# A four-layer hybrid trunk in split fp32: weight remainders and channel sums of the convolution moved to accumulating DMAs, its layer norm shifted by the mean of six blocks within the last block, and several splits reordered

## The chip, the cores and the metric

The kernel runs on one core of one Trainium2 chip. The metric is the device time of one execution in microseconds (us), median of several; less is better. The profile is one execution of its own.

## The reference, cut to what matters

Four layers over 528 tokens (16 meta tokens and 512 of the sequence) of 1024 channels. Each adds a mixer and a gated FFN to `h`; layers 0 and 3 mix by trailing means ("pool"), layer 1 by differential attention, layer 2 by a convolution with a layer norm, which most of the change is about:

```python
def conformer_conv(h, w_in, b_in, dw_w, dw_b, ln_g, ln_b, w_out, b_out):
    a, gate = jnp.split(h @ w_in + b_in, 2, axis=-1)
    u = a * jax.nn.sigmoid(gate)
    u = jnp.pad(u, ((0, 0), (CONV_WIDTH - 1, 0), (0, 0)))          # 31 taps, causal, per channel
    u = lax.conv_general_dilated(u, dw_w[:, None, :], window_strides=(1,), padding='VALID',
                                 dimension_numbers=('NWC', 'WIO', 'NWC'),
                                 feature_group_count=D_MODEL) + dw_b
    u = jax.nn.silu(layernorm(u, ln_g, ln_b))                     # mean and variance over 1024 channels
    return u @ w_out + b_out
...
for i in range(DEPTH):
    h = h + mixer(rmsnorm(h, norm_mix_g[i]))
    h = h + swiglu_ffn(rmsnorm(h, norm_ffn_g[i]), ffn_w_gate[i], ffn_w_up[i], ffn_w_down[i])
return rmsnorm(h[:, N_META:], final_norm_g)
```

## The kernel before

Activations lie transposed in SBUF: 8 blocks of 128 channels by 528 tokens (`h`, `y_hi`, `y_lo`, `cv`). Each fp32 product is made of three matmuls on rounded halves (hi x hi, hi x lo, lo x hi), so every weight tile (128 x 1024, in a ring of four slots) goes four steps: SyncE loads it into `w_raw` (L580), ScalarE rounds it into `w_hi` (`split_hi`, L1532), VectorE writes the remainder `w_raw - w_hi` into `w_lo` (`split_lo`, L1923, counted by `lo_ready`), and TensorE uses it (`chunk`, L834, counted by `tile_used`). SyncE reloads a slot once its `lo_ready` has come, ScalarE writes `w_hi` once TensorE has used the tile before.

The order of the work on each engine is written out by hand, and each engine runs its own program in order. For the convolution (`conv_in`, 8 channel blocks, 2 tiles each) the programs are, per block c:

- TensorE (`pair_layer`): two tiles of matmuls for block c+1, the second after `cv_ready` says that VectorE has read the banks of block c-1, then `convolve(c)` (L948): `TENSOR_TAPS` taps as banded matmuls, 6 per step, taps + 1 steps.
- VectorE (`conv_block`): the two `split_lo` for the next block; `cv_gate` and `cv_a` out of PSUM (L2521, L2523); `u` (L2526); the other 31 - 16 = 15 taps as one multiply-add each (L2534 to L2540, n = 0 to 14, even n into `cv`, odd n into `cv_odd`); `u_lo` behind n = 3 (L2544); behind n = 9 `add_products` of the block before (L2510, L2513), which counts `cv_ready`; at last cv + cv_odd (L2551). The last block has 20 taps on TensorE and 11 on VectorE.
- ScalarE (`conv_gate`): two `split_hi`, `swap_odd` of an earlier block (L1865), the diagonal tap matrices, two instructions of 64 columns per tap (L1852), the sigmoid (L1856), `u_hi` (L1859).
- GpSimd: adds each finished `cv` block into `cv_sum` (L811), seven times.

Layer norm: TensorE sums `cv_sum` and the eighth block over the channels (L1488, L1492), VectorE makes the mean and subtracts it from the eight blocks (L2565), ScalarE squares them (L1544), TensorE sums the squares per token by matmuls with one column (`sum_squares`, L861; two pairs of squares are added on VectorE first), VectorE makes the reciprocal root (L1968 to L1981), TensorE spreads it over the partitions (L868), VectorE copies it (`rstd`, L1986) and scales the blocks (L2577), ScalarE makes silu and `cv_hi`, VectorE `cv_lo` (L2573), and TensorE starts `conv_out`. `fill(n)` issues n matmuls whose result nobody reads, while TensorE would wait.

In the pool layers TensorE multiplies five tiles of rows with the weights (`rows_times_weights`, L892), ScalarE and VectorE split the results (`z_hi` L1591, `z_lo` L2050), and band matmuls (`windows`, L925 to L932) take the trailing means, which VectorE adds to `h` (L2024). In pool0 ScalarE adds a bias to the eight blocks of `h` (L1579), two behind each of the first four `z_hi`.

## Time and profile before

| | us |
|---|---|
| median of 3 runs | 2093.11 (2092.19 to 2095.8) |
| the profiled execution, its own time | 2090.65 |
| its span, first to last instruction | 2088.7 |

TensorE is busy in 97% of the span, VectorE in 76%, ScalarE in 41%, GpSimd in 11%. TensorE's clock is granted at full speed in most of the span and at half of it in some stretches; the mean is 0.983. The stages in order: pool0 until about 73, FFN 0 until 428, attention until 741, FFN 1 until 1094, the convolution until 1326, FFN 2 until 1689, pool3 until 1740, FFN 3 and the output until the end. A row of the timeline is one instruction, or several alike (x2), with start and duration; in brackets stands how long its engine had been idle before it and who ended that.

### The profile page before, as it was taken

To read this page: it belongs to the slowest core of one execution; us is meant where nothing else is said; L and a number is where in the kernel's file an instruction comes from. 1 tells how busy PE (TensorE), PEld (TensorE's weight loads), DVE (VectorE), ACT (ScalarE), POOL (GpSimd) and SP (SyncE) were. 2 spreads that over 40 slices of the span, in tenths; PEclk is the share of its full clock that TensorE was granted. 3 is DMA by queue.
4 is the path that set the end of the run, shared out by engine and by line. 5 is a ranking of instruction groups with operands and counts; after the bars stand their busy time and mean duration, and the time that the engine had idled before them with its cause. 6 is when DMAs were issued, how large, how long until landed. Compare 5 with 4: busy or idle time off the path is not lost.

```text
span 2088.7 us, 40727 instructions
## 1 busy us (share of the span) xinstructions
PE 2030.6 (97%) x16046; PEld 1957.5 (94%) x16046; DVE 1595.3 (76%) x2289; ACT 864.8 (41%) x1359; POOL 221.1 (11%) x309
## 2 busy tenths in 40 slices
PE   7999999999998999999999999999999999999998
PEld 6999999989886999999998999999999988999997
DVE  6797778767777579777978996587787867977794
ACT  6443334334444234333446554243443433433342
POOL 5100000412211400000050001100000061000000
PEclk8999999999998999999999999999999989999999
DMA  5333333331121132333332121223423422333332
GB/s 162 127 88 101 94 107 96 90 110 51 51 60 51 52 91 84 104 96 100 96 107 62 41 61 41 81 82 102 120 84 97 118 76 62 101 101 100 100 102 91
DMA packets 301914, 184.86 MB, mean 89 GB/s; under 512 B 6666, under 2 KB 297483, under 8 KB 301540
## 3 DMA queue, kind: packets, MB, share of 16 engines
q1 hardware_dynamic: 299932, 175.08, 29.2%
q10 hardware_dynamic: 1192, 4.34, 0.5%
q0 software_dynamic: 672, 3.80, 0.5%
q8 instruction: 82, 1.34, 0.3%
q14 instruction: 36, 0.29, 0.0%
HBM read 179.44 MB, written 6.44 MB: 89 GB/s over the span
## 4 chain that ended last, share of the span: by engine, by line
PE 85%; DVE 7%; DVEq 4%; ACT 2%; issue 2%; SPq 0%; DMA 0%; ACTq 0%
PE ps L834 42%; PE ps L1095 35%; DVEq L2539 3%; PE ps L1206 2%; DVE cv L2540 1%; PE ps L1297 1%; PE ps L1273 1%; DVE w_lo L1923 1%; PE ps L932 1%; PE ps L892 1%; DVE scores L2313 0%; PE ps L861 0%; PE ps L1284 0%; PE ps L1308 0%; DMA w_raw<-in_pool_w 0%
## 5 line engine op out<-in xcount | busy, mean ns | idle before, releaser
L1095 PE MATMUL ps<-t_lo,y_hi 128*128 128x264 f32 (+1 forms) x1008 | 285.7, 283 | 0.0
L1095 PE MATMUL ps<-t_lo,w_hi 128*128 128x264 f32 (+1 forms) x1008 | 285.7, 283 | 0.0
L1095 PE MATMUL ps<-t_hi,w_lo 128*128 128x264 f32 (+1 forms) x1008 | 285.4, 283 | 0.0
L1095 PE MATMUL ps<-t_hi,y_lo 128*128 128x264 f32 (+1 forms) x1008 | 285.3, 283 | 0.0
L1095 PE MATMUL ps<-t_hi,w_hi 128*128 128x264 f32 (+1 forms) x1008 | 285.1, 283 | 0.1
L1095 PE MATMUL ps<-t_hi,y_hi 128*128 128x264 f32 (+1 forms) x1008 | 284.8, 283 | 0.0
L834 PE MATMUL ps<-hid_hi,w_hi 128*128 128x264 f32 (+1 forms) x1184 | 265.2, 296 | 0.5 <-DVE hid_lo L2210 0.5
L834 PE MATMUL ps<-hid_lo,w_hi 128*128 128x264 f32 (+1 forms) x1184 | 264.7, 296 | 0.0
L1646 ACT ACTIVATE w_hi<-w_raw 128x1024 fp32r<-128x1024 f32 (+1 forms) x108 | 127.8, 1201 | 329.9 <-PE ps L834 193.6
L834 PE MATMUL ps<-hid_hi,w_lo 128*128 128x264 f32 (+1 forms) x1184 | 264.2, 296 | 0.0
L834 PE MATMUL ps<-y_hi,w_hi 128*128 128x264 f32 (+1 forms) x1088 | 246.3, 303 | 15.7 <-DVE cv L2513 9.2
L834 PE MATMUL ps<-y_lo,w_hi 128*128 128x264 f32 (+1 forms) x1088 | 236.6, 294 | 0.0
L834 PE MATMUL ps<-y_hi,w_lo 128*128 128x264 f32 (+1 forms) x1088 | 235.8, 294 | 0.0
L834 PEld LDWEIGHTS ps<-y_hi,w_hi 128*128 128x128 f32 x1088 | 172.7, 191 | 27.7 <-issue 14.8
L1646 ACT ACTIVATE y_hi<-w_raw 128x1024 fp32r<-128x1024 f32 (+1 forms) x108 | 125.8, 1196 | 166.6 <-DVE w_raw L2164 133.9
L834 PEld LDWEIGHTS ps<-hid_hi,w_hi 128*128 128x128 f32 x1184 | 187.2, 188 | 6.6 <-DVE hid_lo L2210 0.9
L834 PEld LDWEIGHTS ps<-hid_lo,w_hi 128*128 128x128 f32 x1184 | 187.6, 188 | 5.5
L834 PEld LDWEIGHTS ps<-hid_hi,w_lo 128*128 128x128 f32 x1184 | 187.4, 188 | 5.6
L1095 PEld LDWEIGHTS ps<-t_hi,w_hi 128*128 128x128 f32 x1008 | 189.8, 188 | 0.6 <-DVE h L2250 0.5
L1095 PEld LDWEIGHTS ps<-t_hi,y_hi 128*128 128x128 f32 x1008 | 189.8, 188 | 0.0
L1095 PEld LDWEIGHTS ps<-t_lo,w_hi 128*128 128x128 f32 x1008 | 189.5, 188 | 0.1
L1095 PEld LDWEIGHTS ps<-t_hi,w_lo 128*128 128x128 f32 x1008 | 189.5, 188 | 0.0
(315 smaller groups left out, 4435.0 us busy)
## 6 DMA issues: line engine op xcount, KB each, us to landing
w_raw<-in_ffn_w_gate SPq DMA_DIRECT2D x88, 512.0 KB, 5.1
w_raw<-in_ffn_w_up SPq DMA_DIRECT2D x88, 512.0 KB, 4.7
w_raw<-in_ffn_w_down SPq DMA_DIRECT2D x70, 512.0 KB, 4.3
w_raw<-in_ffn_w_down SPq DMA_DIRECT2D x24, 384.0 KB, 4.3
w_raw<-in_attn_w_qkv SPq DMA_DIRECT2D x16, 512.0 KB, 3.8
w_raw<-in_conv_w_in SPq DMA_DIRECT2D x16, 512.0 KB, 4.1
w_raw<-in_attn_w_qkv SPq DMA_DIRECT2D x16, 256.0 KB, 2.9
w_raw<-in_attn_w_o SPq DMA_DIRECT2D x8, 512.0 KB, 3.8
```

What stands on the lines that cost most here:

```text
L834: mm = pe.matmul(ps[:, bank + hf, 0:half], w[:, slot, col:col + P], x(hf), start=begin and w is m.w_hi and n == 0, stop=end and w is m.w_lo)
L892: mm = pe.matmul(out, y[:, at:at + rows], w[:, (t0 + g) % SLOTS, k * 256:(k + 1) * 256], start=k == 0 and n == 0, stop=k == 1 and n == 2)
L932: mm = pe.matmul(out[:, c0:c1], z, m.bands[0:TILE_ROWS[i], g, at:at + c1 - c0], start=i == 2 and n == 0, stop=i in (1, 4) and n == 1)
L1095: mm = pe.matmul(ps[:, bank, 0:hw], w[:, at:at + P], b[:, t, k, 0:hw], start=k == 0 and n == 0, stop=k == 3 and n == 2)
L1206: mm = pe.matmul(bank, x, w, start=False, stop=k == LAST_F - 1 and n == 2)
L1273: mm = pe.matmul(ps[:, (4, proj_banks(par, 1))[part] + c, col:col + k1 - k0], q[rows, q0:q0 + P], k[rows, k0:k1], start=n == 0, stop=n == 2)
L1297: pe.matmul(ps[:, 4, q0:QT * P], v[0:rows, vi, :], w, start=n == 0 and x == 0, stop=n == QT and x == 2)
L1646: act.activation(hi[:, sub * SUB:(sub + n_sub) * SUB], src, ACT.Copy).then_inc(s.op_hi, 1)
L1923: dve.tensor_tensor(m.w_lo[:, slot, 0:n], m.w_raw[:, slot, 0:n], m.w_hi[:, slot, 0:n].bitcast(F32), ALU.subtract).then_inc(s.lo_ready, 1)
L2539: dve.drain()
L2540: dve.scalar_tensor_tensor(out=sums[n % 2], in0=u, scalar=vec_col(ROW_DW + tap, c), in1=sums[n % 2], op0=ALU.mult, op1=ALU.add)
```

## The change

What it does, part by part:

1. **Remainders by DMA in `conv_in`** (16 tiles). ScalarE writes the negated rounded weights into `w_lo` (`negative_hi`), and GpSimd issues a DMA that adds `w_raw` to them (`add_raw`); it waits for both, and counts `lo_ready`. VectorE's `split_lo` is left out there (`split=False`).
2. **Channel sums by DMA.** GpSimd's adds into `cv_sum` become accumulating DMAs (`add_channels`), of six blocks; three pairs of squares are added likewise.
3. **Taps**: 15 on TensorE and 16 on VectorE in blocks 0 to 6 (16 and 15 before), 23 and 8 in the last (20 and 11 before). `add_products` stands behind n = 5.
4. **Layer norm**: the mean of blocks 0 to 5 is subtracted from blocks 0 to 6 within the last block (`centre_early`) and squared there by ScalarE; behind it block 7 is shifted, and an exact correction of variance and mean follows (`ln_factors`, `centre(c)` ahead of each scaling). TensorE's fills are 10 and 26.
5. **Around it**: in `conv_out` both first tiles of FFN 2 are split at block 6, one of them at block 7 before; in the last round of `down2` all four weight tiles of pool3 are split, two before.
6. **pool0**: TensorE takes the first three tiles of rows weight group by weight group; ScalarE has two of the eight biases between the `z_hi` and the rest behind them; some splits and the first `y_lo` stand elsewhere.

```diff
-TENSOR_TAPS = 16
-LAST_TAPS = 20
+TENSOR_TAPS = 15
+LAST_TAPS = 23
...
-LN_SINGLE = 4
-LN_SUMS = tuple(range(LN_SINGLE)) + tuple(range(LN_SINGLE, NB, 2))
+LN_EARLY = NB - 2
+LN_SUMS = tuple(range(0, LN_EARLY, 2)) + tuple(range(LN_EARLY, NB))
+SHIFTS0 = 32
...
@@ gpsimd @@
-            with pool.Fori(0, NB - 1) as d:
-                pool.wait_ge(s.cv_ready, d + 1)
-                pool.tensor_tensor(m.cv_sum[:, :], m.cv_sum[:, :], blk(m.cv, d), ALU.add).then_inc(s.cv_summed, 1)
-                pool.drain()
+
+            def add_channels(c):
+                pool.wait_ge(s.cv_ready, c + 1)
+                if c > 0:
+                    pool.wait_ge(s.cv_added, 16 * c)
+                pool.dma_start(m.cv_sum[:, :], blk(m.cv, c), accum_op=ALU.add).then_inc(s.cv_added, 16)
+            def add_raw(c):
+                for n in range(2):
+                    slot = (first["conv_in"] + 2 + n) % SLOTS if c % 2 == 0 else (first["conv_in"] + n) % SLOTS
+                    pool.wait_ge(s.negated, 2 * c + n + 1)
+                    pool.dma_start(m.w_lo[:, slot, :], m.w_raw[:, slot, :], accum_op=ALU.add).then_inc(s.lo_added[n], 16)
+                for n in range(2):
+                    pool.wait_ge(s.lo_added[n], 16 * (c + 1))
+                    pool.drain().then_inc(s.lo_ready, 1)
+            pool.wait_ge(s.lo_ready, first["conv_in"] + 2)
+            for c in range(NB):
+                add_raw(c)
+                if c > 1:
+                    add_channels(c - 2)
+            for d in range(0, LN_EARLY, 2):
+                pool.wait_ge(s.square_ready, squares_before(R_LN) + d + 2)
+                pool.dma_start(blk(m.cv_square, d), blk(m.cv_square, d + 1), accum_op=ALU.add)\
+                    .then_inc(s.square_pairs, 16)
...
@@ tensor: sum_squares @@
+                def columns_of(src, d, at, pitch):
+                    for n, t in enumerate((0, 128, 256, 384, TOK - P)):
+                        col = at + n * pitch
+                        mm = pe.matmul(ps[:, 5, col:col + 1], blk(src, d, t, P), m.ones[:, 0:1], start=True, stop=True)
+                    return mm
+                pe.wait_ge(s.square_pairs, 16 * (LN_EARLY // 2))
                 for j, d in enumerate(LN_SUMS):
-                    if d < LN_SINGLE:
+                    if d >= LN_EARLY:
+                        pe.wait_ge(s.cv_centred, d + 1)
+                        columns_of(m.cv, d, SHIFTS0 + d - LN_EARLY, 2)
                         pe.wait_ge(s.square_ready, squares_before(R_LN) + d + 1)
-                    else:
-                        pe.wait_ge(s.square_pairs, (d - LN_SINGLE) // 2 + 1)
-                    for n, t in enumerate((0, 128, 256, 384, TOK - P)):
-                        at = n * len(LN_SUMS) + j
-                        mm = pe.matmul(ps[:, 7, at:at + 1], blk(square, d, t, P), m.ones[:, 0:1], start=True, stop=True)
+                    mm = columns_of(square, d, j, len(LN_SUMS))
                 mm.then_inc(s.token_sums, 1)
+                for d in range(LN_EARLY, NB):
+                    for hf in range(2):
+                        mm = pe.matmul(ps[:, 2 + hf, 0:HALF], m.ones[:, :], blk(m.cv, d, hf * HALF, HALF),
+                                       start=d == LN_EARLY, stop=d == NB - 1)
+                mm.then_inc(s.cv_shifts, 1)
...
@@ tensor: pool_layer, rows of the first layer @@
-                    for i in range(TILES):
+                    for g in range(4):
+                        for i in range(3):
+                            rows_times_weights(i, (g,))
+                    for i in range(3, TILES):
...
@@ tensor: pair_layer, end of conv_in @@
+                    pe.wait_ge(s.cv_added, 16 * LN_EARLY)
+                    for hf in range(2):
+                        mm = pe.matmul(ps[:, hf, 0:HALF], m.ones[:, :], m.cv_sum[:, hf * HALF:(hf + 1) * HALF],
+                                       start=True, stop=True)
+                    mm.then_inc(s.cv_sums, 1)
...
@@ tensor: main @@
-            pe.wait_ge(s.cv_summed, NB - 1)
...
-            fill(22)
             sum_squares(m.cv_square)
-            fill(14)
+            fill(10)
...
@@ scalar @@
+            def negative_hi(t):
+                act.activation(m.w_lo[:, t % SLOTS, :], m.w_raw[:, t % SLOTS, :], ACT.Copy, scale=-1.0)\
+                   .then_inc(s.negated, 1)
...
-                for c in (2, 3):
-                    split_hi(tile0 + c, 0, 0, cols[tile0 + c])
                 if name == "pool0":
                     act.wait_ge(s.vec_ready, 1)
                     for d in range(NB):
                         y_hi(d, H_IN, Y_POOL0, ROW_MIX + 0, 0, TOK)
+                        if d in (1, 3):
+                            split_hi(tile0 + (3 + d) // 2, 0, 0, cols[tile0 + (3 + d) // 2])
...
-                    if i < TILES - 1 and name == "pool0":
-                        add_bias(2 * i)
-                        add_bias(2 * i + 1)
+                    if i in (1, 2) and name == "pool0":
+                        add_bias(i - 1)
                 for c in (4, 5):
                     split_hi(tile0 + c, 0, 0, cols[tile0 + c])
+                if name == "pool0":
+                    add_bias(2)
                 for d in range(NB):
                     y_hi(d, hn, yn, row, 0, TOK)
                     act.activation(blk(m.x_square, d), blk(m.h, d), ACT.Square).then_inc(s.square_ready, 1)
+                    if name == "pool0" and d + 3 < NB:
+                        add_bias(d + 3)
...
+                rounds(f"down{layer}", NB, 1, 2, lambda d: y_hi(d, hn, yn, row, 0, TOK),
+                       given={2: [(pool3 - 4, 512), (pool3 - 3, 512)], 3: [(pool3 - 2, 512), (pool3 - 1, 512)]}
+                       if layer == 2 else None)
...
-            rounds("conv_in", NB, 2, NB // 2, conv_gate, True)
+            rounds("conv_in", NB, 2, NB // 2, conv_gate, True, negate=True)
             act.wait_ge(s.conv_done, NB - 1)
             swap_odd(NB - 2, 0)
             for g in (2, 3):
                 split_hi(first["conv_out"] + g, 0, 0, SLOT)
+            squares(s.cv_centred, 0, m.cv, m.cv_square, 0, NB - 1)
             act.wait_ge(s.conv_done, NB)
             swap_odd(NB - 1, 1)
-            squares(s.cv_centred, 0, m.cv, m.cv_square)
+            squares(s.cv_centred, 0, m.cv, m.cv_square, NB - 1, NB)
...
-            rounds("conv_out", NB, 1, 2, conv_out, True, 2)
+            rounds("conv_out", NB, 1, 2, conv_out, True, 2, {2: [(first["up2"] - 4 + c, SLOT) for c in range(2)], 3: []})
...
@@ vector @@
-                for d in range(NB):
-                    if d < 2:
-                        split_lo(tile0 + 4 + d, 0, 0, cols[tile0 + 4 + d])
+                split_lo(tile0 + 4, 0, 0, cols[tile0 + 4])
+                add_windows(0)
+                split_lo(tile0 + 5, 0, 0, cols[tile0 + 5])
+                y_lo(0, yn, row, 0, TOK)
+                for d in range(1, NB):
                     add_windows(d)
-                    if d > 0:
+                    if d > 1:
                         y_lo(d - 1, yn, row, 0, TOK)
...
+                    return
+                pool3 = first["pool3"]
+                out_rounds(f"down{layer}", 1, 2, half, t0, None, yn, row, (0, 2, 4, 6),
+                           given={2: [(pool3 - 4, 512), (pool3 - 3, 512)], 3: [(pool3 - 2, 512)]},
+                           before_low=lambda: split_lo(pool3 + 3, 0, 0, 512))
...
+            def centre(c):
+                return dve.tensor_tensor(blk(m.cv, c), blk(m.cv, c), m.cv_mean[:, :], ALU.subtract)
+            def centre_early():
+                dve.wait_ge(s.cv_sums, 1)
+                dve.tensor_scalar(halves(m.cv_mean[:, :]), banks(0, HALF), 1.0 / (LN_EARLY * P), None, ALU.mult)
+                dve.drain()
+                for c in range(LN_EARLY + 1):
+                    centre(c).then_inc(s.cv_centred, 1)
+            def ln_factors():
+                n = 5
+                x, t = m.tok_x[:, 0:n], m.tok_t[:, 0:n]
+                dve.wait_ge(s.token_sums, R_LN + 1)
+                for sums, at, k in ((x, 0, len(LN_SUMS)), (t, SHIFTS0, NB - LN_EARLY)):
+                    dve.tensor_reduce(out=sums, in_=ps[:, 5, at:at + n * k].rearrange("p (n j) -> p n j", j=k),
+                                      axis=mybir.AxisListType.X, op=ALU.add)
+                dve.drain()
+                dve.tensor_scalar(x, x, 1.0 / D, LN_EPS, ALU.mult, ALU.add)
+                dve.scalar_tensor_tensor(out=t, in0=t, scalar=-1.0 / (D * D), in1=t, op0=ALU.mult, op1=ALU.mult)
+                dve.drain()
+                dve.tensor_tensor(x, x, t, ALU.add)
+                rsqrt(x, m.tok_r[:, 0:n], n)
...
+                dve.wait_ge(s.cv_shifts, 1)
+                dve.tensor_scalar(halves(m.cv_mean[:, :]), banks(2, HALF), 1.0 / D, None, ALU.mult)
+                dve.drain()
+                centre(0)
+                dve.wait_ge(s.rstd_sums, spreads(R_LN) + 1)
+                dve.tensor_copy(halves(m.rstd[:, :]), banks(6, HALF)).then_inc(s.rstd_ready, 1)
+                dve.drain()
...
-                    if n == 9 and not (isinstance(c, int) and c == 0):
+                    if n == 5 and not (isinstance(c, int) and c == 0):
                         add_products(c - 1, 1 - par)
+                        if isinstance(c, int) and c == NB - 1:
+                            dve.drain()
+                            centre_early()
...
-            rounds("conv_in", NB, 2, NB // 2, conv_block, conv_start)
+            rounds("conv_in", NB, 2, NB // 2, conv_block, conv_start, split=False)
             dve.drain()
             add_products(NB - 1, 1)
+            dve.drain()
+            centre(NB - 1).then_inc(s.cv_centred, 1)
+            dve.wait_ge(s.lo_ready, first["conv_out"] + 2)
             split_lo(first["conv_out"] + 2, 0, 0, SLOT)
-            dve.wait_ge(s.cv_sums, 1)
-            dve.tensor_scalar(halves(m.cv_mean[:, :]), banks(4, HALF), 1.0 / D, None, ALU.mult)
-            dve.drain()
-            for c in range(NB):
-                dve.tensor_tensor(blk(m.cv, c), blk(m.cv, c), m.cv_mean[:, :], ALU.subtract)\
-                   .then_inc(s.cv_centred, 1)
-            for d in range(LN_SINGLE, NB, 2):
-                add_squares(R_LN, d // 2, m.cv_square)
-            rstd_of(R_LN, LN_EPS, before_copy=lambda: split_lo(first["conv_out"] + 3, 0, 0, SLOT))
+            split_lo(first["conv_out"] + 3, 0, 0, SLOT)
+            ln_factors()
...
+                if c + 1 < NB:
+                    centre(c + 1)
+                    dve.drain()
...
-            out_rounds("conv_out", 1, 2, HALF, 0, ROW_CONV_OUT, Y_FFN2, ROW_FFN + 2, (0, 2, 4, 6), 2)
+            out_rounds("conv_out", 1, 2, HALF, 0, ROW_CONV_OUT, Y_FFN2, ROW_FFN + 2, (0, 2, 4, 6), 2,
+                       {2: [(first["up2"] - 4 + c, SLOT) for c in range(2)], 3: []})
```

## Rows read from the trace of the kernel before

**Rows 1.** The page, busy time of each engine.
```profile
PE 2030.6 (97%) x16046; PEld 1957.5 (94%) x16046; DVE 1595.3 (76%) x2289; ACT 864.8 (41%) x1359; POOL 221.1 (11%) x309
```

**Rows 2.** Busy by stretch (PE, PEld, DVE, ACT, POOL), then clock, DMA share, GB/s.
```profile
1103.40:1241.50 138.10, 128.78 (x1304) 125.89 (x1304) 126.70 (x173) 84.92 (x273) 9.00 (x6) 0.96 0.16 46
...
1173.00:1174.00 1.00, 1.00 (x6) 1.00 (x6) 1.00 (x1) 1.00 (x5) 1.00 (x1) 0.50 0.00 0
...
1241.50:1277.80 36.30, 33.68 (x340) 32.21 (x337) 29.57 (x56) 13.59 (x21) 2.41 (x2) 0.91 0.21 59
```

**Rows 3.** Timeline of VectorE, one block in the loop.
```profile
1180.95 0.71 DVE L2521 TENSOR_TENSOR cv_gate<-ps,rstd 128x528 f32<-128x528 f32 x1
...
1187.90 0.76 DVE L2540 SCALAR_TENSOR_TENSOR cv_odd<-cv_u,vec,cv_odd 128x528 f32<-128x528 f32 x1
...
1193.31 1.88 DVE L2540 SCALAR_TENSOR_TENSOR cv<-cv_u,vec,cv 128x528 f32 x1 [0.19 <-issue]
...
1199.12 2.35 DVE L1923 TENSOR_TENSOR w_lo<-w_raw,w_hi 128x1024 fp32r<-128x1024 f32 x2
1201.51 0.71 DVE L2521 TENSOR_TENSOR cv_gate<-ps,rstd 128x528 f32<-128x528 f32 x1
```

**Rows 4.** Timeline of GpSimd: the same block, and the issue of a DMA.
```profile
1193.30 1.32 POOL L811 TENSOR_TENSOR cv_sum<-cv_sum,cv 128x528 f32<-128x528 f32 x1 [19.23 <-DVE cv L2513]
...
1661.84 0.62 POOL L816 DMA_DIRECT2D bands<-bands_scratch  x1 [333.20 <-PE ps L834]
```

**Rows 5.** Timeline of TensorE, from about the same block.
```profile
1172.70 0.62 PE L834 MATMUL ps<-y_hi,w_hi 128*128 128x264 f32 x2 [1.93 <-DVE cv L2513]
...
1180.26 0.39 PE L948 MATMUL ps<-u_hi,tap_hi 64*128 64x264 f32 x2
...
1186.74 0.51 PE L834 MATMUL ps<-y_hi,w_hi 128*128 128x264 f32 x2
...
1193.26 0.51 PE L834 MATMUL ps<-y_hi,w_hi 128*128 128x264 f32 x2 [0.40 <-DVE cv L2513]
```

**Rows 6.** Timeline of ScalarE, the same block, and the last block's sigmoid.
```profile
1184.10 2.02 ACT L1532 ACTIVATE w_hi<-w_raw 128x1024 fp32r<-128x1024 f32 x2
...
1187.65 0.35 ACT L1852 ACTIVATE tap_hi<-diag,vec_hi 128x64 fp32r<-128x64 f32 x1
...
1195.09 0.34 ACT L1852 ACTIVATE tap_lo<-diag,vec_lo 128x64 fp32r<-128x64 f32 x1
...
1242.21 0.74 ACT L1856 ACTIVATE cv_sig<-cv_gate,vec 128x528 f32<-128x528 f32 x1 [3.73 <-DVE cv_gate L2521]
```

**Rows 7.** The view of DMA issues: KB each, us from issue to landing.
```profile
w_raw<-in_conv_w_in SPq DMA_DIRECT2D x16, 512.0 KB, 4.1
...
bands<-bands_scratch POOLq DMA_DIRECT2D x1, 1598.0 KB, 7.5
```

**Rows 8.** Timeline of TensorE and VectorE in the layer norm.
```profile
1260.51 8.60 PE L861 MATMUL ps<-ones,cv_square 128*128 128x1 f32 x60
...
1269.14 0.19 DVE L1968 TENSOR_REDUCE tok_x<-ps 128x5 f32<-128x30 f32 x1 [3.83 <-PE ps L861]
...
1273.87 0.71 DVE L1986 COPY rstd<-ps 128x528 f32<-128x528 f32 x1
...
1277.81 0.48 PE L834 MATMUL ps<-cv_hi,w_hi 128*128 128x264 f32 x2 [0.83 <-DVE cv_lo L2573]
```

**Rows 9.** TensorE at the start of FFN 2 (timeline).
```profile
1326.88 0.48 PE L834 MATMUL ps<-y_hi,w_hi 128*128 128x264 f32 x2 [2.04 <-issue]
```

**Rows 10.** TensorE's waits over the span: us in total, times, longest; here pool3.
```profile
PE ps L892 <- DVE w_lo L1923: 2.1, 2, 1.4
```

**Rows 11.** Timeline of pool0: TensorE, ScalarE, TensorE.
```profile
19.67 0.55 PE L892 MATMUL ps<-w_hi,y_hi 128*128 128x256 f32 x1 [5.36 <-DVE y_lo L1929]
...
27.90 1.35 ACT L1579 ACTIVATE h<-h,pool_bs 128x528 f32<-128x528 f32 x2
...
43.71 0.78 PE L834 MATMUL ps<-y_hi,w_hi 128*128 128x264 f32 x2 [0.31 <-DVE y_lo L1929]
```

78 lines of the change are left out of this document (36 added, 42 removed).

## The prediction

> **What bounds the kernel now.** I read the page first: TensorE is busy in 97% of the span [rows 1], so time can only come from stretches in which it waits, works at the lower clock, or does work that this change takes away. The busy time by stretch, read next, shows where the change works: the seven intervals between the gates of the eight convolution blocks take 138.1 us, or 19.7 each, and in them VectorE is busy 126.7 us, nearly as long as TensorE; the layer norm behind them takes 36.3 us until `conv_out` starts [rows 2].
>
> The timelines of one block say who leads. VectorE takes 20.56 us from gate to gate, with no wait but short drains [rows 3]. TensorE waits for VectorE's `add_products` in every block, 1.93 us in one and 0.40 in the next, and after the long wait its granted clock is 0.50, the 1.2 GHz level [rows 2, 5]. Its own work in a block is two tiles of 6.1 us each (6.52 less the wait of 0.40) and a convolution of 6.48 us, together 18.7 [rows 5]. So VectorE sets the pace, and its slack to TensorE is about 1.9 us a block.
>
> **The convolution blocks.** VectorE loses the two remainders, 2.39 us with their overhead (1199.12 to 1201.51) [rows 3]. It loses a stall too: the multiply-add behind `add_products` takes 1.88 instead of 0.76 us, and starts with GpSimd's add (1193.31, 1193.30; the add takes 1.32), so the add costs VectorE 1.12 us a block [rows 3, 4]. It gains one tap, 0.76. That gives 20.56 - 2.39 - 1.12 + 0.76 = 17.8 us. TensorE loses one step of 17 in the convolution, 0.38 us: 18.7 - 0.4 = 18.3. `add_products` moves from behind n = 9 to behind n = 5: at 7.7 us into the block (1188.66, the end of the row at 1187.90) and 1.3 us long it is over at 9.0, and TensorE asks for it 12.2 us in (6.1 of convolution, 6.1 of a tile). That wait goes, and the slow clock with it. What is late next is TensorE itself. From the first gate, two tiles (12.2) and six blocks of 18.3 make 122; VectorE's own, 138.1 - 7 x 2.39 - 6 x 1.12 + 7 x 0.76, would make 120 [rows 2, 3]. 122 against 138.1 is **-16 us**.
>
> What takes over the removed work: ScalarE gets two negations of about 1 us each (as the two roundings, 2.02) and gives back two tap instructions, 0.48. It has some 7 us of idle time ahead of a sigmoid in these blocks and 3.7 in the last one [rows 6], so seven blocks hide it. Its order costs little: `swap_odd` comes at about 7.9 us, ahead of the 8.6 at which the last third of `add_products` wants it. GpSimd's DMAs: nothing in this trace shows an accumulating one. From below they cost nothing, for they have from 7 us (both negated) until TensorE wants the tile in the next block at 18.3 + 6.1 = 24.4, that is 17 us, and nobody but SyncE's reload (4.1 us of slack use) is queued behind `lo_ready`. The nearest rows are a plain load of 512 KB, 4.1 us, and GpSimd's own of 1598 KB, 7.5 [rows 7]. If an accumulation moves twice the bytes, a pair takes 6 to 9 us: hidden. I take nothing. The wait that `add_raw` adds holds back only `add_channels` of two blocks before, which is wanted in the last block.
>
> The Trainium skill ("DMA: Bandwidth & Descriptors", Anatomy of one DMA) prices a DMA from GpSimd at 2.0 us and its bytes at 436 GB/s, an estimate of 3.2 us for 512 KB; it gives no price for adding. By it the sum stays as it is.
>
> **The last block and the layer norm**, counted from the gate of block 7; before: 36.3 us to the first matmul of `conv_out`. ScalarE is 3.4 us later with its taps (negations 2.0, six instructions more at 0.24, 1.4), and the interval is about 1.1 us shorter, against a slack of 3.73 [rows 6]: the sigmoid is about 0.8 late. n = 5 and `add_products` end at 9.0, mean and seven subtractions at 0.63 take 5.1 to 14.1, the last square but one is there at about 15, and the pair sums by DMA at 18 (3 us each, overlapping; between 2 and 7). TensorE, with 24 steps at 0.38 behind 6.9, is free at 16 and waits. It then has 35 column sums where it had 30; those took 8.6 us, 0.29 each, the early ones faster and the last at the lower clock [rows 8]. Block 7's square is there by 19, so TensorE bounds this too: 18 + 9 = 27, and before it was 27.6 (1269.14 less 1241.5). VectorE's two `split_lo` lie under it. From there to the copy of `rstd` it was 4.7 us; now a second reduction and the correction add 0.6, mean and subtraction of block 0 ahead of the copy add 1.4, and a `split_lo` that stood there leaves, its 1.2 having been partly hidden: 5.5. From copy to first matmul it was 3.9 [rows 8]; three more subtractions with drains on VectorE ahead of the first `cv_lo` add 2.1, less 0.35 of waiting: 5.6. 27 + 5.5 + 5.6 = 38.1, or **+2 us** with nothing for a lower clock at the start of `conv_out`. The same gap of 1 to 3 us on TensorE can cost that too: after 1.93 us of waiting the clock was at 1.2 GHz and the tile took 7.56 us (1172.70 to 1180.26) instead of 6.1, a loss of 1.4 [rows 2, 5]. Bounds: -3 (pair sums early, column sums at full clock) and +6.
>
> **FFN 2's start.** TensorE stood 2.04 us for the second tile, split after block 7's add [rows 9]. Split at block 6 it is there a whole block earlier, and TensorE has all else, so this goes whole: **-2 us** (0 if VectorE, which only adds and splits there, were late with it).
>
> **pool3.** Two waits for remainders, 2.1 us together [rows 10], go, and with them a slow clock behind them (up to 1.4 more). But next late is GpSimd's sum of squares, which starts late there, behind the landing of its own DMA. **-2 us**, between 0 and -4.
>
> **pool0.** Six of the eight biases, 1.25 us per two with the overlap taken off [rows 11], leave the chain of `z_hi`: 3.8 us. But the fifth `z_hi` needs TensorE's last row tile, and that comes earlier only by TensorE's earlier start: it stood until 19.67 for `y_lo` [rows 11], and VectorE comes to it about 1.8 us sooner. So the chain gives about 2; `y_lo` of block 0, ahead of the second window add and not behind it, gives about 1.5 more at 43.71, where TensorE waits for it [rows 11]. **-3.5 us**, between -1.5 and -5.5.
>
> **The sum**: -16 + 2 - 2 - 2 - 3.5 = -21.5. The profiled execution took 2090.65, so it would be 2069.2; the median of the runs lies 2.46 above it, which gives 2071.6.
>
> **The rivals.** (1) *The issues take VectorE's port as the add did.* GpSimd issues three DMAs a block, 0.62 us each by the one issue in the trace [rows 4]. If VectorE stands still for them as it did for the add [rows 3], its block is 17.8 + 1.9 = 19.7, 1.4 over TensorE's, seven times: +10, 2081. For it: the stall of 1.12 beside the add. Against it: the issue reads no tensor. The Trainium skill ("SBUF — State Buffer", Who interferes with whom) has VectorE's instructions with two SBUF inputs contend only with a GpSimd instruction that reads SBUF. By that rule this rival costs nothing, and the stall beside the add, which reads, agrees.
>
> (2) *Slower: the accumulating DMAs set the pace.* GpSimd runs them in one queue: a pair, its waits, then the channel sum, about a quarter of a pair's bytes. With 2 us for issues and drains a block takes 2 + 1.25 D, D being the pair. Hidden while D is under 13 us. The other parts save 5.5, so the kernel is slower than before once a block takes over 19.7 + 0.8 = 20.5, D = 15 us or 7.4 us a tile. At D = 20 a block takes 27, and the kernel is (27 - 19.7) x 7 - 5.5 = 45 us slower: 2139. For it: no accumulating DMA is in the trace, and none of 512 KB from SBUF to SBUF. Against it: 1598 KB in 7.5 us, and only 16% of the DMA engines used in the stretch [rows 2, 7].
>
> (3) *The convolution gives more*: if the 6.1 of a tile holds some slack and VectorE leads, the blocks give -19, and the layer norm nothing back: 2066.
>
> (4) *The early shift brings nothing or less*: pair sums late (each at 7 us) and a slow clock at `conv_out`, +6 instead of +2, and pool0 and pool3 give half: 2079.
>
> **How the numbers follow.** Forecast (2066 to 2077) 0.55; (1) 0.12; (3) 0.10; (4) 0.14; (2) 0.09, of which 0.03 is a D just about 14 us that ends within 0.2% of before. 0.2% is about what a measurement of this kernel can tell from no change. Faster 0.91, same 0.03, slower 0.06. The range goes from 2063 (rival 3 with pool0 at its best) to 2084 (rival 1 with half of the small gains).
>
> **What would show it.** Gate to gate at 18.0 to 18.6 us, TensorE without waits for `cv` in the blocks and its clock at 1.0; multiply-adds of VectorE all at 0.77 (1.2 or more beside an issue: rival 1); accumulations of 512 KB landing in 3 to 6 us, and no wait of TensorE for `w_lo` (over 7 us: rival 2); gate of block 7 to `conv_out` at 36 to 40 us, column sums ending at about 27. The prediction fails if an accumulating DMA is much slower than a plain one, or if TensorE in the shorter blocks meets a wait that is hidden now.

## The result, and the profile after

The changed kernel takes 2074.24 us (median of 4 runs, 2073.35 to 2076.54) against 2092.65 of the kernel before: a ratio of 0.9913, 95% interval 0.9896 to 0.993. The forecast was 2071.6, the range 2063 to 2084. Its profiled execution took 2073.5, span 2071.6 (before 2090.65 and 2088.7). In the profile the change is worth 17.1 us where 21.5 were forecast. The median hides 1.7 of that gap by luck: it lies 0.7 us above the profiled execution, where the forecast had added the 2.46 of the kernel before.

The total also hides errors that partly cancel: 8.5 us too little in one row, 4.1 more than forecast over the others. By the same instruction in both traces, in us ("products" are the matmuls of L1095 before and L1141 after, TensorE's longest runs in each FFN):

| stretch | before | after | difference | predicted |
|---|---|---|---|---|
| start to the first product of FFN 0 | 126.36 | 120.70 | -5.7 | -3.5 |
| FFN 0, attention, FFN 1, start of conv_in | 977.03 | 976.55 | -0.5 | 0 |
| gate of block 0 to gate of block 7 | 138.08 | 122.12 | -16.0 | -16 |
| gate of block 7 to conv_out's first matmul | 36.34 | 46.81 | +10.5 | +2 |
| conv_out, head of FFN 2, to its second products | 186.53 | 184.06 | -2.5 | -2 |
| rest of FFN 2, pool3, head of FFN 3, to its second products | 396.72 | 393.70 | -3.0 | -2 |
| sum | | | -17.1 | -21.5 |

The page, then busy time by stretch (columns as in [rows 2]): the blocks, the last block up to the end of its convolution, the column sums, and from there to `conv_out`.

```profile
PE 2022.0 (98%) x16010; PEld 1951.4 (94%) x16010; DVE 1578.2 (76%) x2287; ACT 878.4 (42%) x1367; POOL 233.4 (11%) x327
```

```profile
1097.25:1219.37 122.12, 120.62 (x1254) 118.79 (x1256) 108.97 (x165) 96.15 (x277) 17.10 (x20) 1.00 0.62 138
1219.37:1235.40 16.03, 16.00 (x242) 15.20 (x238) 14.08 (x23) 10.55 (x22) 2.57 (x3) 1.00 0.31 62
1239.05:1254.18 15.13, 15.13 (x71) 15.13 (x72) 1.90 (x3) 1.59 (x2) 0.00 (x0) 0.50 0.25 70
1254.18:1266.18 12.00, 9.26 (x48) 8.12 (x49) 9.88 (x29) 4.21 (x6) 0.54 (x1) 0.82 0.00 0
```

In the blocks TensorE is busy 120.6 of 122.1 us at clock 1.00, where it was busy 128.8 of 138.1 at 0.96 [rows 2]. Behind them, 15.1 us pass with TensorE at the 1.2 GHz level and VectorE all but idle (busy 1.9): there most of the loss against the forecast lies.

VectorE's wait in the first block, then one block of the loop (timeline; answers [rows 3]), and GpSimd's part in one; then the view of DMA issues.

```profile
1100.14 0.77 DVE L2611 SCALAR_TENSOR_TENSOR cv_u<-cv_a,vec,cv_sig 128x528 f32<-128x528 f32 x1 [1.56 <-ACT cv_sig L1904]
...
1166.83 0.71 DVE L2606 TENSOR_TENSOR cv_gate<-ps,rstd 128x528 f32<-128x528 f32 x1
1168.58 0.77 DVE L2611 SCALAR_TENSOR_TENSOR cv_u<-cv_a,vec,cv_sig 128x528 f32<-128x528 f32 x1 [0.42 <-ACT cv_sig L1904]
...
1174.47 0.87 DVE L2595 TENSOR_TENSOR cv<-ps,cv 64x264 f32 x2
...
1175.97 0.77 DVE L2625 SCALAR_TENSOR_TENSOR cv<-cv_u,vec,cv 128x528 f32 x1 [0.19 <-issue]
...
1184.80 0.71 DVE L2606 TENSOR_TENSOR cv_gate<-ps,rstd 128x528 f32<-128x528 f32 x1
```

```profile
1154.43 0.86 POOL L827 DMA_DIRECT2D w_lo<-w_raw  x1 [9.21 <-ACT w_lo L1584]
1156.32 0.86 POOL L827 DMA_DIRECT2D w_lo<-w_raw  x1 [1.03 <-ACT w_lo L1584]
1162.58 0.86 POOL L820 DMA_DIRECT2D cv_sum<-cv  x1 [5.40 <-DMA w_lo<-w_raw]
```

```profile
w_raw<-in_conv_w_in SPq DMA_DIRECT2D x16, 512.0 KB, 4.3
w_lo<-w_raw POOLq DMA_DIRECT2D x16, 512.0 KB, 5.4
...
cv_sum<-cv POOLq DMA_DIRECT2D x6, 264.0 KB, 6.6
cv_square<-cv_square POOLq DMA_DIRECT2D x3, 264.0 KB, 4.3
```

Gate to gate is 17.97 us where it was 20.56. Every multiply-add takes 0.77, the first one behind `add_products` too (1.88 before [rows 3]). An adding DMA of 512 KB lands in 5.4 us, and a pair is there 8.2 us after its first issue (1154.43 to 1162.58). The Trainium skill ("DMA: Bandwidth & Descriptors", Anatomy of one DMA), from which the prediction took an estimate of 3.2 us, falls short of it for an adding DMA; here the measurement decides, and the difference is hidden either way.

The layer norm, TensorE and VectorE (timeline; answers [rows 8]):

```profile
1239.05 6.56 PE L885 MATMUL ps<-ones,cv_square 128*128 128x1 f32 x30 [3.68 <-DMA cv_square<-cv_square]
1245.47 2.27 PE L885 MATMUL ps<-ones,cv 128*128 128x1 f32 x10
1247.60 2.27 PE L885 MATMUL ps<-ones,cv_square 128*128 128x1 f32 x10
1249.73 2.27 PE L885 MATMUL ps<-ones,cv 128*128 128x1 f32 x10
1251.87 2.27 PE L885 MATMUL ps<-ones,cv_square 128*128 128x1 f32 x10
1254.00 3.87 PE L898 MATMUL ps<-cv,ones 128*128 128x264 f32 x8
1254.18 0.18 DVE L2563 TENSOR_REDUCE tok_x<-ps 128x5 f32<-128x25 f32 x1 [13.23 <-PE ps L885]
1260.32 0.71 DVE L2580 COPY rstd<-ps 128x528 f32<-128x528 f32 x1 [0.90 <-PE ps L906]
1266.18 0.48 PE L862 MATMUL ps<-cv_hi,w_hi 128*128 128x264 f32 x2 [2.74 <-DVE cv_lo L2657]
```

The 35 column sums stand in 70 rows (two each), ten of which take 2.13 us from start to start: 0.43 us a sum. They start 19.7 us behind the gate of block 7 (1239.05 less 1219.37) and end at 34.6; the prediction had 18 and 27.

### The profile page after: what moved, and what is told of

The parts are those of the page before. It is cut to its first block, busy times and chain, and to the rows that moved or that the text cites. A ratio compares the mean times of both kernels' runs of the same rounds, so it can differ in the third digit from the quotient of the medians.

```text
span 2071.6 us, 40663 instructions
## 1 busy us (share of the span) xinstructions
PE 2022.0 (98%) x16010; PEld 1951.4 (94%) x16010; DVE 1578.2 (76%) x2287; ACT 878.4 (42%) x1367; POOL 233.4 (11%) x327
## 4 chain that ended last, share of the span: by engine, by line
PE 78%; DVE 8%; DVEq 4%; ACT 3%; issue 3%; POOLq 1%; DMA 1%; SPq 0%; ACTq 0%; POOL 0%
PE ps L862 38%; PE ps L1141 31%; DVEq L2624 2%; PE ps L1252 2%; PE ps L930 1%; PE ps L1343 1%; PE ps L1319 1%; DVE w_lo L1972 1%; PE ps L885 1%; PE ps L973 1%; DVE cv L2625 1%; DVE w_lo L2198 1%; DVEq L2234 1%; POOLq L750 1%; DVEq L2203 1%
## 5 line engine op out<-in xcount | busy, mean ns | idle before, releaser
L1141 PE MATMUL ps<-t_lo,y_hi 128*128 128x264 f32 (+1 forms) x1008 | 285.8, 284 | 0.0
L1141 PE MATMUL ps<-t_lo,w_hi 128*128 128x264 f32 (+1 forms) x1008 | 285.8, 284 | 0.0
L1141 PE MATMUL ps<-t_hi,w_lo 128*128 128x264 f32 (+1 forms) x1008 | 285.5, 283 | 0.0
L1141 PE MATMUL ps<-t_hi,y_lo 128*128 128x264 f32 (+1 forms) x1008 | 285.4, 283 | 0.0
L1141 PE MATMUL ps<-t_hi,w_hi 128*128 128x264 f32 (+1 forms) x1008 | 285.2, 283 | 0.0
L1141 PE MATMUL ps<-t_hi,y_hi 128*128 128x264 f32 (+1 forms) x1008 | 284.9, 283 | 0.0
L1141 PEld LDWEIGHTS ps<-t_hi,w_hi 128*128 128x128 f32 x1008 | 189.9, 188 | 0.6 <-DVE h L2294 0.5
L1141 PEld LDWEIGHTS ps<-t_hi,y_hi 128*128 128x128 f32 x1008 | 189.9, 188 | 0.0
L1141 PEld LDWEIGHTS ps<-t_lo,w_hi 128*128 128x128 f32 x1008 | 189.6, 188 | 0.1
L1141 PEld LDWEIGHTS ps<-t_hi,y_lo 128*128 128x128 f32 x1008 | 189.5, 188 | 0.0
L1141 PEld LDWEIGHTS ps<-t_hi,w_lo 128*128 128x128 f32 x1008 | 189.5, 188 | 0.0
```

The costliest lines, as they stand in the source:

```text
L1141: mm = pe.matmul(ps[:, bank, 0:hw], w[:, at:at + P], b[:, t, k, 0:hw], start=k == 0 and n == 0, stop=k == 3 and n == 2)
```

## The experiments

The distance that most runs turn on, from the gate of block 7 to the first matmul of `conv_out`, was read from each run's timeline:

| run | median, us | ratio to before, 95% | gate 7 to conv_out |
|---|---|---|---|
| before | 2092.65 | | 36.34 |
| changed | 2074.24 | 0.9913 (0.9896 to 0.993) | 46.81 |
| e1_fill_ahead | 2076.3 | 0.9925 (0.9909 to 0.9942) | 45.28 |
| e2_unpaired | 2074.63 | 0.9918 (0.9901 to 0.9934) | 46.95 |
| e3_chain | 2070.44 | 0.9901 (0.9885 to 0.9918) | 40.37 |
| e4_old_ln | 2065.44 | 0.9878 (0.9861 to 0.9894) | 37.80 |
| e5_split_vector | 2090.8 | 0.9992 (0.9983 to 1.0002) | 42.84 |
| e6_add_gpsimd | 2080.54 | 0.9943 (0.9927 to 0.996) | 44.60 |
| e7_taps14 | 2079.78 | 0.9945 (0.9927 to 0.9963) | 44.54 |
| e8_spread_old | 2080.73 | 0.9951 (0.9935 to 0.9968) | 45.72 |
| e9_dma_twice | 2083.27 | 0.9955 (0.9938 to 0.9971) | 43.45 |
| e10_keep_pool3 | 2062.81 | 0.9852 (0.9836 to 0.9869) | 39.26 |
| e11_keep_ln | 2062.06 | 0.9859 (0.9843 to 0.9876) | 37.65 |
| e12_early_few | 2067.84 | 0.9887 (0.9871 to 0.9904) | 43.09 |

The runs e5 to e9 have the changed kernel's layer norm as it is, and the distance still runs from 42.84 to 46.81 with it. Their column sums start 18.4 to 20.7 us behind the gate and take 11.3 to 15.0, by the instant at which the clock falls: e8, which starts them behind the same wait as the changed kernel (3.69 us), takes 13.6. Differences under 4 us there are not to be read as effects. Each group of runs was measured beside the kernel before, whose median moved between 2091.2 and 2092.7, so medians of different rows compare to some 1.5 us.

### The layer norm: where do the 10.5 us come from?

**e4_old_ln**: the changed kernel with the layer norm of before.

```diff
-LAST_TAPS = 23
+LAST_TAPS = 20
-LN_SUMS = tuple(range(0, LN_EARLY, 2)) + tuple(range(LN_EARLY, NB))
+LN_SUMS = tuple(range(LN_SINGLE)) + tuple(range(LN_SINGLE, NB, 2))
-                            centre_early()
+            add_channels(NB - 2)
...
```

> The changed kernel with the layer norm of the kernel before: mean of all eight blocks, 20 taps in the last block, six column sums a group, the channel sum still by DMAs. What the early shift costs or gives by itself. My prediction put it at +2 us of 38.3; the trace of the changed kernel has 46.8 from gate 7 to conv_out. If the early shift itself is the loss (theory A), this kernel takes 35.5 to 37.5 us there (36.3 in the kernel before, TensorE with one step less in block 6, ScalarE later with the taps) and the whole kernel is 9 to 11 us faster than the changed one: 2064. Rival E, the loss comes from what the other edits brought into that stretch (DMAs of GpSimd, the late sigmoid, the shorter block ahead of it): 42 us or more here too, and the kernel is no more than 5 us faster.

37.80 us, just over theory A's 37.5, and 8.8 us faster in the median. The early shift itself is the loss, and not what the other edits brought into the stretch (rival E wanted 42 or more).

```profile
1238.11 10.16 PE L887 MATMUL ps<-ones,cv_square 128*128 128x1 f32 x60
...
1256.98 0.48 PE L860 MATMUL ps<-cv_hi,w_hi 128*128 128x264 f32 x2 [0.83 <-DVE cv_lo L2663]
```

With the gate at 1219.18 its column sums end at 28.95 us (34.63 in the changed kernel, 5.7 later), and from there to `conv_out` it takes 8.85 (12.2, 3.3 more). So two thirds of the loss lies ahead of the last column sum and one third behind it.

**e1_fill_ahead**: matmuls that nobody reads fill the wait for the pair sums; 1.04 us of it are left behind them.

```diff
+            pe.wait_ge(s.cv_centred, 1)
+            fill(30)
             sum_squares(m.cv_square)
```

> The changed kernel, with 30 matmuls that nobody reads between the last convolution and the column sums, where TensorE stands 3.68 us for the pair sums. Counted from the gate of block 7 to the first matmul of conv_out (46.8 us in the changed kernel). Theory A, the lower clock after that wait is what costs: the clock stays at 1.0 into the column sums, they take 7 to 9 us where they took 15.1, and the interval is 39 to 41, the kernel 6 us faster. Rival B, column sums of one column let the clock fall whatever ran ahead of them: they take 14 us or more and the interval stays at 46 to 47.5. Rival C, they are slow for another reason than the clock (their own weight loads, the DMA beside them): the clock shows 1.0 and they still take 0.43 us each.

45.28. TensorE's clock, by slices (TensorE busy, clock, DMA share, GB/s):

```profile
1239.00:1242.00 3.00, 3.00 (x26) 1.00 1.02 172
1242.00:1246.00 4.00, 2.96 (x27) 1.00 0.28 73
1246.00:1250.00 4.00, 4.00 (x30) 0.75 0.66 198
1250.00:1254.00 4.00, 4.00 (x21) 0.50 0.00 0
```

The sums began at 1244.07 (20.9 us behind the gate, 1.2 later than in the changed kernel), at full clock, and lost it within 4 us although nothing interrupted them (TensorE is busy 4.00 of 4.00 us in both of the last slices); all 35 took 11.4 us instead of 15.0. At full clock a sum takes 0.22 us (the first 15 in 3.37). Neither theory A's 39 to 41 nor rival B's "14 us or more" came out, and rival C is excluded, for the duration follows the clock. A full clock ahead of the sums is kept for their first part only.

**e2_unpaired**: no pair sums by DMA, 50 column sums.

```diff
-            for d in range(0, LN_EARLY, 2):
-                pool.wait_ge(s.square_ready, squares_before(R_LN) + d + 2)
-                pool.dma_start(blk(m.cv_square, d), blk(m.cv_square, d + 1), accum_op=ALU.add)\
-                    .then_inc(s.square_pairs, 16)
-LN_SUMS = tuple(range(0, LN_EARLY, 2)) + tuple(range(LN_EARLY, NB))
+LN_SUMS = tuple(range(NB))
```

> The changed kernel without the three adding DMAs for the pairs of squares: TensorE sums the columns of all eight squares one by one, 50 column sums where it had 35, and has no DMA to wait for, so that it starts behind the last convolution, some 4 us earlier. Theory A (clock): from a start without a wait the sums run the first part at full clock, 0.21 us each, and then drop to 0.43; 50 of them at a mean of 0.3 are 15, and the interval from the gate of block 7 to conv_out is 43 (-4 us). Rival B (clock always low in these sums): 50 x 0.43 = 21.5 us from 16.5, the interval is 49.5 (+2.7). Rival D, the landing of the DMA is the whole loss: -3.7 us and more.

46.95, between theory A's 43 and rival B's 49.5. The sums began at 15.9 us, 3.75 earlier, and ended at 35.2: 19.2 us for 50, the clock at 0.50 from 1242 on. The DMA's landing is not the loss (rival D falls); what it bought, fifteen sums less, was worth just what its wait cost.

**e3_chain**: VectorE adds the squares of blocks 3 to 6 while it is idle.

```diff
+            for a, b in ((3, 4), (5, 6), (3, 5)):
+                e = dve.tensor_tensor(blk(m.cv_square, a), blk(m.cv_square, a), blk(m.cv_square, b), ALU.add)
-LN_SUMS = tuple(range(0, LN_EARLY, 2)) + tuple(range(LN_EARLY, NB))
+LN_SUMS = (0, 1, 2, 3, NB - 1)
```

> The changed kernel without the adding DMAs of squares; VectorE, which stands 13.2 us there, adds the squares of blocks 3 to 6 in three additions (2.1 us), and TensorE has 35 column sums as in the changed kernel, the first 25 without a wait right behind the convolution. Theory A (clock kept by an early start): sums from 16.5 us behind the gate, 35 x 0.25 to 0.3 = 9 to 10.5, done at 26 to 27 where the changed kernel is done at 34.6: the interval is 38 to 40 and the kernel 7 us faster. Rival B (clock low whatever comes ahead): 35 x 0.43 = 15 us from 16.5, done at 31.5, the interval 43.7, 3 us faster.

```profile
1235.29 4.02 PE L881 MATMUL ps<-ones,cv_square 128*128 128x1 f32 x30
1239.17 4.41 PE L881 MATMUL ps<-ones,cv 128*128 128x1 f32 x20
1243.43 4.41 PE L881 MATMUL ps<-ones,cv_square 128*128 128x1 f32 x20
```

40.37, just over theory A's 40. But the sums took 12.4 us, between its 9 to 10.5 and rival B's 15: the first 15 ran mostly at full clock, 3.9 us; the other 20 took 8.5, 0.43 each. 6.4 us came back, 3.7 of them from the earlier start and 2.5 from the clock. In the profile 3.0 us of that are lost again in pool3 (42.6 us there where the changed kernel has 39.6); e10 says why.

**e12_early_few**: the early shift with fewer sums, an early start, and the fills of pool3 (e10 below).

```diff
-LN_SUMS = tuple(range(0, LN_EARLY, 2)) + tuple(range(LN_EARLY, NB))
+LN_SUMS = (0, 1, 2, NB - 1)
...
+                        for _ in range(14):
+                            pe.matmul(ps[:, 0, 0:HALF], m.y_hi[:, 0:P], m.y_hi[:, 0:HALF], start=True, stop=True)
...
+            for a, b in ((2, 3), (4, 5), (2, 6), (2, 4)):
```

> The early shift of the changed kernel, with its column sums arranged as the runs so far suggest: VectorE adds the squares of blocks 2 to 6 (four additions, 2.9 us), TensorE has 30 column sums where the changed kernel has 35, starts them behind the last convolution, runs 14 matmuls that nobody reads ahead of the last ten; pool3 with the added matmuls as in the last two runs. Is the idea at fault or the way its sums are made? Theory (only the sums): they end 25 us behind the gate of block 7 (34.6 in the changed kernel, 28 in the run before), and with the 12.2 us that the changed kernel takes from there conv_out starts at 36 to 37, as early as with the old layer norm or earlier (37.65): about 2061 for the kernel. Rival (the early shift costs by its longer tail and by TensorE's own shift sums, whatever the squares do): 38.5 us or more, the kernel 1 us or more slower than the run before.

43.09, and 2067.84 against the 2062.06 of e11_keep_ln, which differs from it in the layer norm. The sums were done at 30.1 us, not at 25: this time the clock fell 2 us after they began (they start at 1237.88, and its mean from 1239 to 1242 is 0.64), and the 14 added matmuls took 3.2 us at the low clock. From the last sum to `conv_out` it took 13.0. The rival's number holds: even with 30 sums the early shift is behind the old form, which had 20 in e11 and 9.8 us from its last sum to `conv_out`. By these figures 3.2 us of the 5.4 between the two lie in the tail and 2.3 ahead of it.

### The blocks: who leads, and does the DMA hold?

**e5_split_vector**: the remainders back on VectorE, nothing else.

```diff
-            rounds("conv_in", NB, 2, NB // 2, conv_block, conv_start, split=False)
+            rounds("conv_in", NB, 2, NB // 2, conv_block, conv_start)
-                add_raw(c)
...
-                                if negate:
+                                if False:
                                     negative_hi(t)
```

> The changed kernel with the remainders of conv_in split on VectorE again: no negations on ScalarE and no adding DMAs of weights; the rest (15 taps, add_products behind n = 5, channel sum by DMA) stays. Theory (VectorE set the pace, by the prediction's sum): its block is 20.56 - 1.12 + 0.76 = 20.2 us, gate to gate, where the changed kernel has 17.9; six such blocks cost 6 x 2.3 = 14 us, about 2088. Rival (TensorE's waits for add_products were the loss, and its move to n = 5 removes them alone): 18.5 us or less a block and no more than 4 us slower in all.

Gates 20.20, 20.14, 20.15, 20.13 us apart in the loop, where the sum gave 20.2; 136.3 in all against 122.1. TensorE waited for `add_products` again (its waits from 1110 to 1219):

```profile
PE ps L860 <- DVE cv L2596: 8.6, 4, 3.0
```

The move to n = 5 does not remove the waits alone; VectorE set the pace. 14.2 us of the change's 16 hang on the two remainders, and without them hardly anything is left of the whole gain (2090.8, where 2088 was expected).

**e6_add_gpsimd**: the channel sum as GpSimd's addition.

```diff
-                pool.dma_start(m.cv_sum[:, :], blk(m.cv, c), accum_op=ALU.add).then_inc(s.cv_added, 16)
+                pool.tensor_tensor(m.cv_sum[:, :], m.cv_sum[:, :], blk(m.cv, c), ALU.add).then_inc(s.cv_added, 16)
```

> The changed kernel with the sum of the channel blocks as a GpSimd addition again, in place of its DMA. Theory (stall of VectorE): the multiply-add beside the addition takes 1.9 us again where all take 0.77, VectorE's block is 17.8 + 1.1 = 18.9 us by the prediction, 0.6 to 1 us over TensorE's 17.9 to 18.3, so 4 to 6 us slower over six blocks. Rival (VectorE has slack now): the long multiply-add shows and the gates stay 17.9 apart, the kernel within 1 us of the changed one.

```profile
1184.68 1.82 POOL L818 TENSOR_TENSOR cv_sum<-cv_sum,cv 128x528 f32<-128x528 f32 x1 [4.97 <-DMA w_lo<-w_raw]
```

```profile
1185.49 1.59 DVE L2624 SCALAR_TENSOR_TENSOR cv<-cv_u,vec,cv 128x528 f32 x1 [0.17 <-issue]
```

The stall is back, 0.82 us in this block, and the gates are 18.7 to 19.1 apart in the loop: 127.6 in all, 5.5 more. That is VectorE's full price: 0.8 in six blocks is 4.9, so it had no slack to hide it. Beside a DMA issue nothing of the kind shows. The Trainium skill ("SBUF — State Buffer", Who interferes with whom) has it so: a VectorE instruction with two inputs in SBUF contends with what reads SBUF on GpSimd. The traces agree on both sides.

**e7_taps14**: one more tap on VectorE.

```diff
-TENSOR_TAPS = 15
+TENSOR_TAPS = 14
```

> The changed kernel with 14 taps on TensorE in blocks 0 to 6 where it has 15 (VectorE 17 where it has 16): who leads in the blocks now. By the prediction VectorE takes 17.8 and TensorE 18.3 a block; one tap moved makes it 18.6 and 17.9, so VectorE would lead and six blocks cost (18.6 - 17.9 measured) x 6 = 4 us more. Rival (VectorE has more slack than the prediction gave it, TensorE alone sets the pace): 17.5 us a block, 2.3 us faster.

18.8 to 19.2 us a block in the loop, 127.9 in all (+5.8), and TensorE waits (1110 to 1219):

```profile
PE ps L862 <- DVE cv L2598: 3.8, 5, 1.2
```

Seven taps of 0.77 are 5.4, so this too is the full price, over the expected 4: VectorE already led. In the changed kernel TensorE has no wait at all in that stretch, and VectorE none for TensorE, only the 0.42 for the sigmoid. From convolution to convolution TensorE takes 18.05 us; its tiles are done 3.3 us ahead of the gate of block 1 and 0.4 ahead of that of block 7. So at 15 taps VectorE sets the gates, with TensorE just behind it.

**e9_dma_twice**: every adding DMA of a tile doubled.

```diff
+                    pool.dma_start(m.cv_square[:, n * SLOT:(n + 1) * SLOT], m.w_raw[:, slot, :], accum_op=ALU.add)\
+                        .then_inc(s.extra, 16)
+                pool.wait_ge(s.extra, 32 * (c + 1))
```

> The changed kernel with the adding DMAs of the weights doubled: ahead of each, one more of 512 KB adds the same raw tile into the unused buffer of squares, and lo_ready waits for both. The prediction had 17 us between the negations and TensorE's need, and took the DMAs at nothing; they land in 5.4 us. Theory (slack as in the prediction): four transfers instead of two, some 11 to 12 us with the issues, stay hidden; the gates stay 17.9 apart, and only the first block pays, where TensorE waited 2.3 us already and will wait 7 to 8: about 5 us in all. Rival (the slack is nearly used up, a GpSimd queue in the way): TensorE waits for w_lo in every block, 2 us or more each, 14 us and more in all.

TensorE's only wait for a remainder was the first (waits of TensorE, then of VectorE, over the blocks):

```profile
PE ps L868 <- POOLq L834: 8.7, 1, 8.7
```

```profile
DVE cv_gate L2612 <- PE ps L868: 7.3, 4, 4.4
```

The tiles landed 11.1 us after the issue, and in the loop the gates stay 17.9 to 18.3 apart. In all the blocks take 129.6, 7.5 more: 4.5 in the first block, as expected, 1.3 each in the second and the last. Behind the long wait TensorE leads, and VectorE waits for it at four gates, so the 16.7 us of those two blocks become TensorE's 18.05. The wait is 6.4 us longer, and 1.4 come from the clock behind it (13.3 us to the first convolution where the changed kernel takes 11.9). One more wait came with the load: 3.25 us for the channel sum, in the last block. The slack of the prediction holds within the loop, and twice the load is about where it ends.

### The rest of the kernel

**e8_spread_old**: the spread of `rstd` where it was.

```diff
-                                if head and len(pars) == 1 and c == 0 and k == NB - 2:
-                                    spread_rstd(r)
                             if head and par == 1 and c == 1:
+                                if len(pars) == 1:
+                                    spread_rstd(r)
                                 pe.wait_ge(s.rstd_ready, r + 1)
```

> The changed kernel with the spread of rstd in the heads of FFN 0, 2 and 3 back where it was, between the third and the fourth tile of the head, so that TensorE stands again until VectorE has copied rstd (0.80 us at the start of FFN 2 in the kernel before). The prediction had no term for this move. If it gave part of what came on top (pool0 5.7 against 3.5), each head is 0.8 to 1.0 us longer, counted from the sum of tokens to the fourth tile, and the kernel 2.5 to 3 us slower; with a lower clock behind the wait up to 2 us more each. Rival: the wait only takes the place of another one, and nothing changes, within 0.5 us.

From the sum of tokens to the first product, against the changed kernel: FFN 0 +1.2, FFN 2 +1.1, FFN 3 +1.1, together 3.4 us, a little over the theory's 2.5 to 3. The medians are 6.5 apart; the executions of this kernel spread from 2074 to 2084, with the mean granted clock between 0.987 and 0.982. The part of the 6.5 that isn't the 3.4 goes with the clock as far as that mean tells; the profiled execution was the fastest of them, so where it fell in the others isn't shown.

**e10_keep_pool3**: e4 with matmuls that nobody reads in three short waits of pool3.

```diff
+            def keep(bank, n=10):
+                for _ in range(n):
+                    pe.matmul(ps[:, bank, 0:HALF], m.y_hi[:, 0:P], m.y_hi[:, 0:HALF], start=True, stop=True)
+                    keep(4)
                     sum_tokens(r, TILE_STARTS)
...
```

> The changed kernel with the layer norm of the kernel before (as in the fourth run), and with 10 matmuls that nobody reads in each of the three places at pool3 where TensorE stands 1.3 to 1.5 us (for h, for the sums of squares, for the last z_lo). Theory (what costs there is the lower clock behind these short waits): in the fourth run's trace that stretch has the clock at 0.50 from 1689 to 1701 and 0.6 to 0.8 before it; it stays at 1.0, and from the end of down2 to the spread of FFN 3 the kernel is 5 to 8 us faster, less up to 0.5 for the added matmuls. Rival: the clock falls all the same, or the waits grow by what was added; within 1 us.

From the sum of tokens of pool3 to that of FFN 3 (by stretch) in e4, in the changed kernel, in e10:

```profile
1673.46:1716.01 42.55, 41.15 (x220) 36.69 (x221) 23.55 (x33) 19.40 (x25) 19.40 (x17) 0.80 0.09 25
```

```profile
1683.42:1722.98 39.56, 38.15 (x220) 34.04 (x221) 23.90 (x33) 19.42 (x25) 19.41 (x17) 0.87 0.09 27
```

```profile
1679.55:1716.42 36.87, 36.44 (x230) 32.69 (x231) 23.51 (x33) 19.32 (x25) 19.92 (x17) 0.95 0.10 29
```

The same instructions with the same idle time (1.4 us in each) take 39.6 or 42.6 by how long the clock stays down behind it, and 36.9 when the waits are filled; e11 and e12, which have the same fills, take 35.3 each, and of the eight other kernels with this code and no fills none is under 38.0. From the spread of FFN 2 to that of FFN 3 the gain over e4 is 4.7 us, a little under the expected 5 to 8; the kernel is 2.6 us faster in the median, and the intervals overlap (0.9861 to 0.9894 and 0.9836 to 0.9869).

**e11_keep_ln**: e10 with 20 column sums in place of 30, in the old layer norm, and 24 matmuls that nobody reads between the first ten and the last ten (the edit is shown against e10).

```diff
-LN_SUMS = tuple(range(LN_SINGLE)) + tuple(range(LN_SINGLE, NB, 2))
+LN_SUMS = (0, 1, 2, 6)
+            add_squares(R_LN, 1, m.cv_square, 0)
+            dve.tensor_tensor(blk(m.cv_square, 2), blk(m.cv_square, 2), blk(m.cv_square, 4), ALU.add)\
+               .then_inc(s.square_pairs, 1)
```

> The kernel of the run before with fewer column sums in the layer norm: VectorE, which stood 5.19 us for them, adds the squares of blocks 2 to 5 and of 6 and 7, four additions in place of two, so that TensorE has 20 column sums instead of 30, and it runs 24 matmuls that nobody reads between the first ten and the last ten. Theory (column sums are paid by TensorE at the lower clock, and the clock is kept by real matmuls between them): the last column sum ends at 27 us behind the gate of block 7 where it ended at 29, the clock stays at 1.0 there, and conv_out starts 2 to 3 us earlier (35 to 36 us instead of 37.8). Rival (VectorE's additions become the bound): 37.5 us or more.

37.65 where e10 had 39.26 and e4 37.80: no gain that stands out from the differences between executions. The last sum ended at 27.9 us behind the gate, a microsecond earlier than in e4, but the clock was at 0.50 again for part of the way: 1.00 in both groups of sums, and 0.62 and 0.64 on average in the matmuls behind each. The rival's number came (37.5 or more), but not its cause, for TensorE never waits for VectorE's additions. e10 and e11 (2062.81 and 2062.06, not told apart) are the fastest versions here, some 12 us below the changed kernel.

## Why the prediction was right, and where it was wrong

**The blocks: right in size and in what it removed; the 122 itself is partly luck.** 122 was forecast, 122.12 came, and e5 gives the prediction's 20.2 when the remainders return, e6 its stall. But the prediction had TensorE late next, at 12.2 + 6 x 18.3, and VectorE's own sum at 120. TensorE takes 18.05 a block, and VectorE waits for it at no gate: VectorE still leads (e6, e7), and its sum came 2.1 short. Of these 1.4 are a wait for the sigmoid in the first block, 1.56 where the kernel before had 0.19:

```profile
1104.91 0.77 DVE L2526 SCALAR_TENSOR_TENSOR cv_u<-cv_a,vec,cv_sig 128x528 f32<-128x528 f32 x1 [0.19 <-ACT cv_sig L1856]
```

In e5, without ScalarE's negations, that wait is 0.20. So seven blocks do not hide ScalarE's new work, as the prediction said; the first one doesn't. The other 0.7 is 0.1 a block.

**DMAs at nothing: right.** A pair takes 8.2 us against bounds of 6 to 9; e9 shows the slack. One wait wasn't named, though "no wait of TensorE for `w_lo`" was a sign of being right: the first block's second tile, split within `conv_in` itself, keeps TensorE waiting 2.34 us until 1098.75. It is hidden, for VectorE waits for TensorE at no gate behind it. But TensorE's tiles are done only 0.4 us ahead of the gate of block 7, so hardly more would have been.

**The layer norm: wrong, +10.5 for +2, and outside the bounds of -3 and +6.** The failing term is the duration of the column sums. It took 0.29 us each from the 60 rows of before [rows 8] and came to 9 us for 35 (18 + 9 = 27), though the text itself said that the early ones had run faster and the last at the lower clock. A mean over two clock levels is no price: 0.22 and 0.43 are, and the 35 sums came out wholly at 0.43, 15.0 us. That is 6.0 of the 8.7 us missing (46.8 for 38.1). The wait of 3.68 ahead of them can answer for 3 of these 6.0 at most: with a shorter wait or none the first 15 sums took 3.4 us instead of 6.4 at best (e1, e9), and the other 20 took 8.0 to 8.5 in every run, so that no run has 35 sums under 11.3. The start came 1.7 late: the last pair was issued 15.1 us behind the gate and had landed 4.5 us later (3 was taken), and the sigmoid came 1.2 later behind the gate than before, not 0.8. Behind the sums 12.2 us passed where 5.5 + 5.6 was summed, 1.1 more. VectorE stands 0.90 for the spread of `rstd`, which is queued on TensorE behind shift sums that the prediction has no term for (L898, 3.3 us at clock 0.50) and ten fills (1.9 us, at 0.70).

**FFN 2's start: right.** The 2.04 us are gone (58.5 us from the start of `conv_out` to the sum of tokens, 60.8 before), and the spread gives 1.1 more (e8). Between the first and the second products 0.9 are lost again, 65.0 for 64.1; the cause of that was not looked for.

**pool3: right in size, by luck.** -3.0 for -2, of which 1.0 is the spread of FFN 3, which the prediction had left out. The waits for remainders went, 2.15 us. But a wait of 1.29 for GpSimd's sum of squares came, the one the prediction named as next, and that for `h` grew by 0.6, so the waits together give 0.3. The rest is the clock between TensorE's first row of pool3 and the sum of tokens: 5.9 us of work where it was 7.8. And the same code varies by 4.6 us with the clock a little later, from 38.0 in e8 to 42.6 in e3.

**pool0: right, with two things missing.** FFN 0's first matmul starts 3.1 us earlier (40.58 for 43.71), the sum said 3.5. The rest of the 5.7 is the spread (1.2, e8) and the clock (1.3), which the profile of the changed kernel happened to keep:

```profile
40.00:44.00 4.00, 3.72 (x28) 1.00 0.77 223
```

```profile
40.00:44.00 4.00, 4.00 (x19) 0.50 0.83 243
```

The first is the changed kernel, the second e1_fill_ahead, the same code up to there. Its matmul starts within 0.2 us of the other, and the sum of tokens comes at 64.41 instead of 60.18.

**The rivals.** (1), the issues take VectorE's port: refuted, 0.77 throughout. (2), adding DMAs that set the pace: refuted at this load. (3), the blocks give -19: no, although its condition holds, VectorE leads. (4) came nearest: it had the early shift at +6 and a slow clock, but put the clock at the start of `conv_out`, where it was 1.00, and not in the column sums, and it had pool0 and pool3 at half, which came in full.

What stays open: why the clock falls after 4 us of column sums in one execution and after 2 in another (e1, e12), and how far the row differences of one pair of profiles hold for the medians.

## What to carry to other kernels

Price work at the clock level at which it will run: a mean over rows at two levels hides a factor of two, and of a string of one-column matmuls only the first 5 us at most ran at the higher level here, with or without a wait ahead of it. When an engine is relieved, ask whether it still leads: one more unit of work on it then costs its full price, as in e7. Where the vector engine leads and the DMA queues idle, an adding DMA can take a whole subtraction off it, as long as its landing has a block's slack. Fill short waits of the tensor engine only where long matmuls follow, as in pool3; ahead of one-column matmuls it bought little.

## What the runs showed of the hardware

- An adding DMA from GpSimd lands in 5.4 us for 512 KB and 4.3 to 6.6 for 264 KB, SBUF to SBUF (medians of the changed kernel; 11.1 us for 512 KB at twice the load, e9); its issue takes 0.86 us and doesn't slow VectorE.
- A GpSimd addition of 1.82 us beside VectorE's multiply-add stretches that from 0.77 to 1.59 (1.88 in the kernel before).
- Column sums of one column take 0.22 us at full clock and 0.43 at the lower level, and the clock falls in the midst of them without a wait (e1, e3): TensorE being busy in the profile's sense, 4.00 of 4.00 us, did not keep it.
- In pool3 GpSimd's first square stood 6.42 us, and the profile names no releaser. It starts 0.4 us after GpSimd's DMA of 1598 KB, issued just ahead, has landed (1647.77 and 7.2 us); that its drain waits for the landing is inferred from this.
- Executions of the same code differ by 4 us at FFN 0 (19.6 to 23.7 from its first matmul to the sum of tokens) and by 4.6 us in pool3 (38.0 to 42.6 from one sum of tokens to the next), with the granted clock, so a profile's difference of that size needs a second profile.
